# Moving context products, read-outs and the last value products in a two-layer diffusion block

## The reference, cut to what matters

```python
zc = jnp.split(hc @ w_in[l], N_PARTS, axis=-1)      # context, 256 tokens
zx = jnp.split(hx @ w_in[l], N_PARTS, axis=-1)      # sequence, 512 tokens
a_val, a_gate, q, k, v, u, sv, bg, cg, xin = z      # N_PARTS = 10, 256 columns each
p1 = softmax(q1 @ k1.T * scale); p2 = softmax(q2 @ k2.T * scale)
o = (p1 - lam * p2) @ v                             # 4 heads, blocks of 128 queries
y = concat([y_a, y_b, y_c, y_d]) @ w_out
...
if l < DEPTH_2 - 1:                                 # the context goes through the
    h_ctx = h_ctx + mod_c[2] * token_mixers(zc, ...)  # mixers in the first layer only
```

## Time and profile before

| What | Value |
|---|---|
| runs of the kernel | 2115.18, 2118.0, 2124.75 us |
| span of the profiled execution, first to last instruction | 2113.5 us |
| time given for the profiled execution itself | none beside its span |
| PE busy | 2040.2 us, 97% of the span |
| DVE, ACT, POOL busy | 60%, 38%, 3% |
| mean granted TensorE clock | 0.998 |
| DMA | 249 MB, 118 GB/s |

### The profile page before, as it was taken

One profiled execution on the slowest core, in us unless ns is written; L12 is line 12 of the kernel. 1 busy time (PEld: TensorE's weight loads), 2 busy tenths in 40 slices (PEclk: granted clock), 3 DMA queues, 4 the chain that ended last, 5 costly groups with the idle time before them and its releaser, 6 DMA issues.

```text
span 2113.5 us, 26503 instructions
## 1 busy us (share of the span) xinstructions
PE 2040.2 (97%) x11156; PEld 1739.0 (82%) x11156; DVE 1270.3 (60%) x1696; ACT 795.1 (38%) x1117; POOL 72.4 (3%) x81
## 2 busy tenths in 40 slices
PE   6999999999999999999999999999998999999998
PEld 5989888778788888887888888888787787888887
DVE  7466866867657885727546455464689645344343
ACT  4333334584343455534113122132536534132231
POOL 0000000000120000020000000001100010000001
PEclk9999999999999999999999999999999999999999
DMA  8643523525322531222333232232353122232221
GB/s 290 224 159 120 213 86 129 186 90 188 131 100 74 162 92 70 70 82 98 111 111 120 90 120 100 100 122 105 112 167 90 70 90 89 91 100 100 100 95 65
DMA packets 54054, 249.18 MB, mean 118 GB/s; under 512 B 6224, under 2 KB 12512, under 8 KB 35504
## 3 DMA queue, kind: packets, MB, share of 16 engines
q1 hardware_dynamic: 52048, 242.41, 33.4%
q10 hardware_dynamic: 1296, 2.63, 0.3%
q0 software_dynamic: 592, 2.46, 0.3%
HBM read 232.53 MB, written 12.06 MB: 116 GB/s over the span
## 4 chain that ended last, share of the span: by engine, by line
PE 85%; DVE 9%; ACT 3%; issue 2%; DMA 1%; POOL 0%; ACTq 0%; DVEq 0%; POOLq 0%
PE banks L1957 70%; DVE small L1351 2%; PE banks L1981 1%; PE banks L1982 1%; PE banks L1983 1%; PE banks L652 1%; PE banks L531 1%; ACT whi_f L2107 1%; PE banks L643 1%; DVE wlo_f L2317 1%; DVE ntx L2351 1%; PE banks L607 1%; PE banks L606 1%; PE banks L608 1%; PE banks L2013 1%
## 5 line engine op out<-in xcount | busy, mean ns | idle before, releaser
L1957 PE MATMUL banks<-hxh,whi_f 128*128 128x512 f32 (+1 forms) x1464 | 585.4, 400 | 24.3 <-ACT hxh L2136 7.5
L1957 PE MATMUL banks<-hxh,wlo_f 128*128 128x512 f32 (+1 forms) x1464 | 569.7, 389 | 0.0
L1957 PE MATMUL banks<-hxl,whi_f 128*128 128x512 f32 (+1 forms) x1464 | 555.2, 388 | 0.2 <-DVE hxl L2386 0.2
L2317 DVE TENSOR_TENSOR wlo_f<-raw_f,whi_f 128x2048 fp32r<-128x2048 f32 x133 | 304.9, 2293 | 181.4 <-ACT whi_f L2107 181.2
L2107 ACT ACTIVATE whi_f<-raw_f 128x2048 fp32r<-128x2048 f32 x133 | 253.7, 1907 | 308.3 <-PE banks L1957 290.1
L1957 PEld LDWEIGHTS banks<-hxh,whi_f 128*128 128x128 f32 x1464 | 276.1, 189 | 86.6 <-issue 27.5
L1957 PEld LDWEIGHTS banks<-hxh,wlo_f 128*128 128x128 f32 x1464 | 275.8, 188 | 57.9
L1957 PEld LDWEIGHTS banks<-hxl,whi_f 128*128 128x128 f32 x1464 | 274.9, 188 | 58.0 <-issue 1.9
L1957 PE MATMUL banks<-fxh,whi_f 128*128 128x512 f32 (+1 forms) x528 | 205.6, 389 | 2.1 <-DVE cT L1495 1.1
L1957 PE MATMUL banks<-fxh,wlo_f 128*128 128x512 f32 (+1 forms) x528 | 204.2, 387 | 0.0
L1957 PE MATMUL banks<-fxl,whi_f 128*128 128x512 f32 (+1 forms) x528 | 203.5, 385 | 0.0
(11 more groups left out here) (340 smaller groups left out, 3129.3 us busy)
## 6 DMA issues: line engine op xcount, KB each, us to landing
raw_f<-in_wst SPq DMA_DIRECT2D x133, 1024.0 KB, 4.9
mvr<-in_mst SPq DMA_DIRECT2D x120, 512.0 KB, 5.8
stack<-qk_parts SPq DMA_DIRECT2D x36, 192.0 KB, 6.6
x_kept<-xT SPq DMA_DIRECT2D x2, 2048.0 KB, 8.6
raw_f<-in_wst SPq DMA_DIRECT2D x8, 384.0 KB, 5.9
xT<-x_kept SPq DMA_DIRECT2D x2, 1536.0 KB, 8.7
qk_parts<-qk_h SPq DMA_DIRECT2D x3, 768.0 KB, 3.8
qk_parts<-qk_l SPq DMA_DIRECT2D x3, 768.0 KB, 3.6
```

What stands on the lines that cost most here:

```text
L1957: last = pe.matmul(o, (wh, wl)[w][:, k, c, :], r[part][:, k, :], start=(k == order[0] and parts is not LOW and (w, part) == (0, 0)), stop= ...
L2317: dve.tensor_tensor(wlo[r][:], raw[r][:], whi[n % 2 if n > N_FIRST else n][:].bitcast(F32), ALU.subtract).then_inc(w_lo, 1)
```

## The change

On PE, in the first layer, the first half of chunks 6 to 9 does the sequence products of k-steps 0 and 1, then waits for `ctx_out`, then does the context products of both. The value products of unit 19 (places 84 to 89) go to between the first k-step's two halves of the first output chunk. On ACT and DVE the comparison of `upto` becomes `<=`, and ACT's `exp(v)` asks for `p.scores(v) + 2`; neither edit is limited to the first layer. `upto(80)` becomes `upto(79)`.

```diff
-                        if i == 0 and c == 0 and l == 0:
+                        late = l == 0 and c == 0 and i < 2
+                        last = step(n, j % 2, k, c, X if late else own, order, place)
+                        if late and i:
                             pe.wait_ge(ctx_out, j - 5)
-                        last = step(n, j % 2, k, c, own, order, lambda r: ctx_acc[:, c, :] if r[2] else acc[:, c, 0:T])
+                            for k0 in order[:2]:
+                                step(n, j % 2, k0, c, XC[1:], order, place)
...
-            for g in range(80, 90):
+            for g in range(80, 84 if l == 0 else 90):
                 fill(g)
+
+            def last_values():
+                for g in range(84, 90):
+                    fill(g)
...
-                 between={(0, 7): lambda: o_turned(0), (0, 2): lambda: o_turned(1)}, order=Y_ORDER)
+                 between={(0, 7): lambda: o_turned(0), (0, 2): lambda: o_turned(1), **({(1, 4): last_values} if l == 0 else {})},
+                 order=Y_ORDER)
...
             def upto(g):
-                while done[0] + 8 < g and done[0] < 80:
+                while done[0] + 8 <= g and done[0] < 80:
...
             def exp(v, part):
-                upto(p.scores(v))
+                upto(p.scores(v) + 2)
...
-                while done[0] + 8 < g and done[0] < 80:
+                while done[0] + 8 <= g and done[0] < 80:
...
-            upto(80)
+            upto(79)
```

More of the change, by code:

```diff
@@ L762, in layer, with place @@
                 for c in range(2):
+                    def place(r):
+                        return ctx_acc[:, c, :] if r[2] else acc[:, c, 0:T]
                     tail = j == N_WIN - 1 and c == 1
```

## The result

The changed kernel takes 2134.9 us (median of six runs, 2130.3 to 2137.1); the kernel before, run beside it, takes 2118.3 (six runs, 2115.2 to 2124.8). The ratio is 1.0075, with a 95% interval of 1.0063 to 1.0087: slower by 0.75%, 16.7 us, where 9.6 were forecast. The time lies above the range. The profiled execution spans 2134.3 us against 2113.5.

The account below looks back on a forecast made before the run. PE, busy 97% of the span, was taken to bound the kernel. Layer 0 +1.5, layer 1 +6.2 and the clock +1.9 made 9.6 us slower; added to the median of 2118.0, the forecast was 2127.5 us, range 2120 to 2133.

Parts of the forecast that it names:

- The waits, their new owners and their lengths: PE's read-out waits go; stops on ACT come at turn(3) and turn(8) of layer 0, turn(8) and scores(13) of layer 1.
- The order, +7.7 us: Cost of reordering without falls of the clock: +1.5 us in layer 0 and +6.2 in layer 1.
- three large terms: Exponentials delayed behind read-outs or splits: +2.7 us at layer 0's chunk 7, +3.2 and +2.7 at layer 1's units 9 and 12.
- slack: Rival: half of layer 1's two large terms and of chunk 7's made up later; +3.4 without falls, 2121.4 us, chance 0.12.
- The starts of chunks 8 and 9: Layer 0: read-out waits go, -0.8 us at chunk 8 and -1.3 at chunk 9, where unit 15's chain begins sooner.
- The last values, +1.0: Layer 0's end: unit 19's value products, formerly in the shade of a wait, come onto the path; +1.0 us, between 0 and 2.
- The clock, +1.9: PE's clock falls after the two 4.4 us stops: 1.6 us in layer 0, 0.3 at scores(13) of layer 1.
- The two falls that the sum had: Clock falls behind turn(8) of layer 0, 1.6 us, and behind scores(13) of layer 1, 0.3 us.
- Smaller stops, such as the 2.1 us at chunk 6, left the clock at 1.00: Claim from the earlier trace that shorter PE stops cause no fall; only the two 4.4 us stops were priced.
- The third, at up to 1.2, I leave to a rival: A fall behind the 3.9 us stop at turn(8) of layer 1, up to 1.2 us, left out of the sum.
- 0.3 at scores(13): Layer 1: the fall there costs 0.3 us, as PE's waits of 1.4 to 1.7 us in the next units absorb it.
- My rival with all falls in it: Three falls (1.6, 1.2, 0.3 us) and 1.4 more for the table switch: +12.2, 2130.2 us, chance 0.20.

Follow-up runs that it names:

- e1_late_wait: Kernel before with only PE's late wait for ctx_out in the first layer; ACT's and DVE's order and last values as before: 2114.2 us, ratio 0.9973.
- e2_readouts: Kernel before with only the edits of upto and exp on ACT and DVE, in both layers; PE as before: 2133.0 us, ratio 1.0058.
- e7_first_halves: Kernel before with PE's late wait and, on ACT, only first halves' read-outs moved ahead of the exponentials; splits and last values as before: 2115.0 us, ratio 0.9973.
- second profile of the changed kernel: The changed kernel run once more, unaltered, beside a version with two stops filled: 2135.0 us, ratio 1.0069.
- e5_layer1_restored: Changed kernel with the edits of upto and exp in the first layer only, the second layer's order as before: 2123.8 us, ratio 1.0017.

## Why the prediction was wrong

- **The waits, their new owners and their lengths**: right. Four stops forecast at 2.3, 4.4, 3.9 and 4.4 us came at 2.22, 4.24, 3.72 and 4.57.
- **The order, +7.7 us**: right, and in its three large terms one by one. With the stops filled the kernel is 7.5 us over the one before by medians, 5.9 by the ratio. The three large terms (2.7 for chunk 7 of layer 0, 3.2 and 2.7 for units 9 and 12 of layer 1) were measured at 2.8, 3.4 and 2.9. No slack took any of these.
- **The starts of chunks 8 and 9**: right where the clock fell no more than before (-1.1 and -0.5 us against -0.8 and -0.3, the latter with the last values in it).
- **The last values, +1.0**: the mechanism is right. The size is not clear of the noise by runs (+1.2, and the interval includes no change); of the +2.3 in the profiled execution a longer fall holds 1.7.
- **The clock, +1.9**: this is the step that failed. It measured about 8 us by medians, 10 by the ratios. The two falls that the sum had came as priced (chunk 7 of layer 0 is 1.4 us shorter with the stop filled, where 1.6 was forecast, and scores(13) 0.3, where 0.3 was); the two that it left at nothing came at 1.5 (`turn(3)`) and 2.1 us (`turn(8)` of layer 1). Three sentences of it fell. "Smaller stops, such as the 2.1 us at chunk 6, left the clock at 1.00": the one of 2.22 us was followed by a fall. "The third, at up to 1.2, I leave to a rival": the filler there makes chunk 7 of layer 1 2.1 us shorter. And "0.3 at scores(13), as there PE waits 1.4 to 1.7 us in each of the next units and works the loss off" prices a fall by its slack; there the stage did give back most of it (3.2 against 2.9 filled), but the clock fell once more at 1780 us, 1.6 us, in every profile with both late stops of layer 1 unfilled (three) and in none of the other nine. Of the 8 us the filled stages account for 5.5 and this later fall for 1.6; the rest I cannot place.
- **Slips of no weight**: 2118.0 + 9.6 is 2127.6 and not 2127.5, from 1597.72 to 1599.0 is +1.3 and not +1.2, and on ACT five read-outs of half-chunks move in the first layer (both halves of chunks 5 and 6, the first of 7), not four.

The chain of error is one of counting: of four stops I let two count, one at the shortest fall that the trace of before showed and one at 0.3. I told them apart by length, with 2.1 us as harmless, and the trace of before already spoke against that: its one fall ahead of the kernel's last microseconds, at 872 us, came behind a stop of 1.41 us, while none came behind 2.06 at chunk 6. The same stop of 1.41 us stands in three more profiles (e1_late_wait, e2_readouts, e7_first_halves), each time with a fall. The rule on the clock that I cited, from the Trainium skill, "TensorE: Matmul & The Clock Gate", section "What's actually happening", that idling brings the gate to half rate, was told as speaking against the change. The first profile agrees with it at all four stops, the second at three; the sum took it at two. My rival with all falls in it, 2130.2, was still 5 us short, as it priced three and each at 1.6 or less, and 1.4 of it was a price of the table switch that did not come (its load took 1.28 us).

Of the 16.7 us by medians, then: about 8 by the order and about 8 by the clock, to some 2 us either way. Putting the splits back takes the loss away, so they carry nearly all of it. Cut the other way, it is 5 in layer 0 and 11 in layer 1.

What stays open: why the clock falls at 1780 us only when both late stops of layer 1, 90 us earlier, are unfilled. It falls there at the end of a stop of PE:

```profile
1779.90 0.72 PE L1968 MATMUL banks<-hxh,whi_f 128*128 128x512 f32 x1 [2.02 <-DVE wlo_f L2328]
```

All twelve profiles have this stop, at 2.02 to 2.07 us, and nine of them have no fall behind it. No run was made with fillers at the output stage alone, nor one with the splits moved back and the stops filled.

## What to carry to other kernels

On an engine that works in order, moving a cheap read-out ahead also moves what its helper carries behind it: look for the dearest instruction in the moved piece (here a 1.9 us split behind 0.95 us of read-outs) and for who waits for what now stands behind it. A helper that two layers share changes both, so cost the layer with nothing to gain first. And when an edit lengthens stops of PE (here to between 2.2 and 4.6 us), add a fall of the clock for every one; filling a stop with matmuls whose result is overwritten is a cheap test of that share, and here by the medians a gain by itself.

## What the runs showed of the hardware that was not expected

- The stop ahead of `turn(3)`, 2.22 us in the changed kernel and 1.87 with the read-outs alone, was followed by a fall, where 2.1 us had not been in the kernel before. It is not certain: in the second profile of the changed kernel the clock stayed up there. Of the four profiles with that stop three show a fall; behind the stops of 3.7 us and more every one does. Length does not sort the others: behind the 1.41 us ahead of `values(19)` all four profiles that have it show a fall, behind the 2.0 us at 1780 us three of twelve.
- The length of a fall differs between executions of the same kernel: behind `turn(8)` of layer 0 3.4 us in the first profile and 6.8 in the second; in layer 1 the other way round.
- The clock also fell where PE had not stood. In the changed kernel, a stretch inside chunk 8:

```profile
832.00:834.00 2.00, 2.00 (x10) 1.90 (x9) 1.75 (x2) 1.66 (x3) 0.00 (x0) 0.50 0.00 0
```

  Eight of the twelve profiles have such a fall between 817 and 837 us, the kernel before has none. In all eight it begins 1.8 to 4.0 us after the first of 24 matmuls of a single column each:

```profile
827.11 2.84 PE L684 MATMUL banks<-consts,sqm 128*128 128x1 f32 x24 [0.21 <-ACT sqm L1039]
```

  The four profiles without the fall have these matmuls too, so they are at most a part of the cause, and it was not tried. Chunk 8 with such a fall in it is 0.5 us longer than before, without it (e5_layer1_restored) 1.1 shorter.
- 50 matmuls that do nothing made the changed kernel 8 us faster.
